# Sparse attention in a two-block transformer on one core: the selection added on VectorE instead of by an identity matmul, and two PSUM banks exchanged

## The reference, cut to what matters

```python
def dsa_attention(q, k, v, iq, ik, iw, rel_bias, topk):      # per block of 128 queries
    score = jnp.einsum('bqhs,bqh->bqs', jax.nn.relu(s_idx), iwb)
    score = jnp.where(keys <= pos_q, score, -jnp.inf)
    _, idx = lax.top_k(score, topk)                           # topk = 128
    ...
    logits = jnp.einsum('bqhd,bqkd->bhqk', qb, kg) * scale
    logits = logits + bias(pos_q - idx)
    p = jax.nn.softmax(jnp.where(valid, logits, -jnp.inf))
    return jnp.einsum('bhqk,bqkd->bqhd', p, vg)
```

## Time and profile before

| | us |
|---|---|
| median of 3 runs (3006.83 to 3009.97) | 3009.62 |
| profiled execution, whole | 3007.83 |
| its span, first to last instruction | 3006.0 |
| TensorE busy (94% of the span) | 2836.8 |
| VectorE busy (36%) | 1091.3 |
| GpSimd busy (37%) | 1103.3 |
| ScalarE busy (31%) | 927.0 |
| mean granted TensorE clock | 0.969 |

### The profile page before, as it was taken

How to read it: one execution, slowest core, us unless ns; L and a number is a source line. 1 busy time by engine, 2 the same in 40 slices (tenths; PEclk the granted TensorE clock), 3 DMA queues, 4 the chain that set the end, 5 groups by cost and what they waited for, 6 DMA issues and landing times.

```text
span 3006.0 us, 34273 instructions
## 1 busy us (share of the span) xinstructions
PE 2836.8 (94%) x13922; PEld 2176.9 (72%) x13922; DVE 1091.3 (36%) x1796; ACT 927.0 (31%) x1425; POOL 1103.3 (37%) x536
## 2 busy tenths in 40 slices
PE   3679999999998997699999999999999999999999
PEld 1167688878877785357887677766788877777787
DVE  2262133113224402322221447854322465666411
ACT  2031241224124211042222322255422222666411
POOL 3043302341341330024554333444455443445443
PEclk8589999999999998799999999999999999999999
DMA  8914722231238320032434233322344333332442
GB/s 293 351 56 145 228 62 61 68 94 41 71 88 130 84 71 28 14 127 74 123 112 99 70 98 85 91 78 85 123 123 119 84 99 91 85 83 76 137 122 81
DMA packets 459337, 311.94 MB, mean 104 GB/s; under 512 B 32016, under 2 KB 412816, under 8 KB 458416
## 3 DMA queue, kind: packets, MB, share of 16 engines
q1 hardware_dynamic: 425264, 265.41, 30.8%
q10 hardware_dynamic: 33920, 44.37, 5.7%
HBM read 289.71 MB, written 32.10 MB: 107 GB/s over the span
## 4 chain that ended last, share of the span: by engine, by line
PE 89%; DMA 4%; DVE 3%; POOL 2%; ACT 1%; issue 1%; SPq 0%; ACTq 0%; DVEq 0%; POOLq 0%
PE acc L1654 75%; PE aux L1654 7%; PE ssq L1657 3%; PE ssq L1654 3%; DMA ada_ring<-in_w_ada 2%; DMA raw<-in_w_in 1%; POOL normed L1042 1%; DVE x_t L1191 1%; DVE rstd L1222 1%; PE aux L1657 1%; POOL w_lo L1053 1%; DMA masks_sb<-in_masks 1%; ACT staged L727 0%; ACT w_hi L748 0%; DVE p L1283 0%
## 5 line engine op out<-in xcount | busy, mean ns | idle before, releaser
L1053 POOL TENSOR_TENSOR w_lo<-raw,w_hi 128x1024 fp32r<-128x1024 f32 x362 | 869.7, 2403 | 1699.7 <-ACT w_hi L748 1699.7
L1654 PE MATMUL acc<-h_hi,w_hi 128*128 128x512 f32 (+1 forms) x3232 | 1211.0, 392 | 23.4 <-DVE x_t L1191 8.0
L1654 PE MATMUL acc<-h_hi,w_lo 128*128 128x512 f32 (+1 forms) x3232 | 1173.2, 380 | 0.0
L1654 PE MATMUL acc<-h_lo,w_hi 128*128 128x512 f32 (+1 forms) x2464 | 873.0, 376 | 0.8 <-issue 0.8
L748 ACT ACTIVATE w_hi<-raw 128x1024 fp32r<-128x1024 f32 x362 | 383.0, 1059 | 1166.2 <-PE acc L1654 1086.2
L1654 PEld LDWEIGHTS acc<-h_hi,w_hi 128*128 128x128 f32 x3232 | 585.7, 188 | 176.4 <-issue 52.3
L1654 PEld LDWEIGHTS acc<-h_hi,w_lo 128*128 128x128 f32 x3232 | 584.2, 188 | 118.1
L1654 PEld LDWEIGHTS acc<-h_lo,w_hi 128*128 128x128 f32 x2464 | 441.1, 189 | 94.7 <-issue 13.0
L1654 PE MATMUL acc<-out_t_lo,w_hi 128*128 128x512 f32 x768 | 298.9, 389 | 0.0
L1222 DVE RECIPROCAL rstd<-rstd 128x512 f32<-128x512 f32 (+1 forms) x29 | 118.0, 4070 | 407.0 <-ACT rstd L788 407.0
L1654 PEld LDWEIGHTS acc<-out_t_lo,w_hi 128*128 128x128 f32 x768 | 144.3, 188 | 29.1
(11 more groups left out here) (217 smaller groups left out, 2341.1 us busy)
## 6 DMA issues: line engine op xcount, KB each, us to landing
raw<-in_w_in SPq DMA_DIRECT2D x52, 1024.0 KB, 5.8
raw<-in_even_w_in SPq DMA_DIRECT2D x41, 1024.0 KB, 5.5
raw<-in_odd_w_in SPq DMA_DIRECT2D x36, 1024.0 KB, 5.6
ada_ring<-in_w_ada SPq DMA_DIRECT2D x32, 1024.0 KB, 8.7
gate_ring<-in_w_ada SPq DMA_DIRECT2D x16, 1024.0 KB, 7.1
raw<-in_w_out SPq DMA_DIRECT2D x16, 1024.0 KB, 5.9
raw<-in_even_w_out SPq DMA_DIRECT2D x16, 1024.0 KB, 5.8
raw<-in_odd_w_out SPq DMA_DIRECT2D x16, 1024.0 KB, 6.6
```

Source lines behind the costliest of these rows:

```text
L1053: G_.tensor_tensor(WL[half][:], RAW[G.rs][:, half * HALF * P:(half + 1) * HALF * P], WH[half][:].bitcast(F32), ALU.subtract).then_inc(S["l ...
L1654: return M.matmul(out_, lhsT, rhs, start=start, stop=stop, skip_group_check=True)
```

## The change

The selection is no longer added on TensorE. The two matmuls with the fp32r identity, the identity's tile `IDR` and its cast go, and `SEL` becomes plain fp32. For qt > 0 VectorE adds the mask to the scores of both heads in one operation, from PSUM and SBUF into `P2`, with a semaphore `d_picked` for which it then waits itself; the two operations of bias and maximum then read `P2` in place of PSUM. For qt = 0 they read PSUM as before. The scores now go to the two banks of `AUX`, and the values product to the upper halves of `ACC`.

```diff
-    V2, IDR = at("v2_nat", QT * 64, 172 * K1), at("ident_r", P, 173 * K1, F32R)
+    V2 = at("v2_nat", QT * 64, 172 * K1)
-    SEL = at("select_mask", 3 * SEQ, 178 * K1, F32R)
+    SEL = at("select_mask", 3 * SEQ, 178 * K1)
...
                     dve.wait_ge(S["d_out"], u + 1)
-                    Vv.tensor_tensor(o, AUX[:, (u % 2) * 512:(u % 2) * 512 + P], o, ALU.mult).then_inc(S["d_fin"], 1)
+                    Vv.tensor_tensor(o, ACC[:, u % 2, 512:512 + P], o, ALU.mult).then_inc(S["d_fin"], 1)
                 if s < 32:
                     j, qt = DSA_UNITS[s]
                     nk = P * (qt + 1)
                     need(dve, "d_turned", 2 * (s - 4) + 2)
+                    if qt:
+                        p = P2[qt][:].rearrange("p (h n) -> p h n", n=nk)
+                        sel = SEL[:, (qt - 1) * SEQ:(qt - 1) * SEQ + nk].unsqueeze(1).to_broadcast([P, 2, nk])
+                        dve.wait_ge(S["d_scored"], 2 * s + 2)
+                        Vv.tensor_tensor(p, AUX[:].rearrange("p (h n) -> p h n", n=512)[:, :, 0:nk], sel, ALU.add).then_inc(S["d_picked"], 1)
+                        dve.wait_ge(S["d_picked"], 3 * j + qt)
                     for half in range(2):
...
-                        Vv.tensor_tensor_reduce(out=P2[qt][:, half * nk:half * nk + nk], in0=ACC[:, half, 512:512 + nk],
+                        p = P2[qt][:, half * nk:half * nk + nk]
+                        Vv.tensor_tensor_reduce(out=p, in0=p if qt else AUX[:, half * 512:half * 512 + nk],
                                                 in1=TR[slot][:, SEQ - nk:SEQ], scale=-1.0, scalar=-NEG, op0=ALU.add,
                                                 op1=ALU.min, accum_out=LNG[:, c:c + 1]).then_inc(S["d_max"], 1)
...
                     elif k == "ikw":
                         dve.wait_ge(S["y_turned"], 1)
-                        L.done(Vv.tensor_copy(IDR[:], IDENT[:]))
...
-                            e = mm(AUX[64 * half:64 * half + 64, (u % 2) * 512:(u % 2) * 512 + P], V2[:, b * 64:b * 64 + 64],
+                            e = mm(ACC[64 * half:64 * half + 64, u % 2, 512:512 + P], V2[:, b * 64:b * 64 + 64],
...
-                    if qt:
-                        pe.wait_ge(S["sel_done"], 1)
-                        for half in range(2):
-                            mm(ACC[:, half, 512:512 + nk], IDR[:], SEL[:, (qt - 1) * SEQ:(qt - 1) * SEQ + nk], True, False)
                     for half in range(2):
                         rows = slice(64 * half, 64 * half + 64)
-                        mm(ACC[:, half, 512:512 + nk], Q2[rows, j * SEQ + qt * P:j * SEQ + (qt + 1) * P], K2[rows, 0:nk],
-                           qt == 0, True).then_inc(S["d_scored"], 1)
+                        mm(AUX[:, half * 512:half * 512 + nk], Q2[rows, j * SEQ + qt * P:j * SEQ + (qt + 1) * P], K2[rows, 0:nk],
+                           True, True).then_inc(S["d_scored"], 1)
```

More of the change, by code:

```diff
@@ L492, in build @@
             "i_scored", "i_relu", "i_acc",
-            "d_scored", "d_max", "d_exp", "d_inv", "d_norm", "d_turned", "d_pt0", "d_pt1", "d_out", "d_fin",
+            "d_scored", "d_picked", "d_max", "d_exp", "d_inv", "d_norm", "d_turned", "d_pt0", "d_pt1", "d_out", "d_fin",
             "w_scored", "w_max", "w_exp", "w_inv", "w_norm", "w_turned", "w_pt0", "w_pt1", "w_out", "w_fin")}
```

## The result

The changed kernel takes 3016.07 us (median of 7 runs, 3012.96 to 3020.16) against 3009.56 us (7 runs). The ratio is 1.0024, 95% interval 1.0013 to 1.0036: about 0.24% slower. A second measurement on another occasion gave 1.0025 (1.0016 to 1.0034).

What follows compares the result with a forecast made beforehand. TensorE bounds the kernel (89% of the chain), with VectorE already last to arrive once per gate group. 5.8 - 4.2 + 8.9 - 0.5 + 1.7 = +11.7 us on the profiled 3007.83 gives 3019.5; stated 3020.5 us, range 3004 to 3033.

Steps and rivals of the forecast that it cites:

- the likeliest case: The forecast itself: VectorE comes late at hooks 12 and 4, 3020.5 us, own range 3016 to 3025, chance 0.47.
- Removal, 1.64 us a group: TensorE's selection matmuls in the eight gate groups go: 13.1 us in all if nothing else were late.
- Hook 8 to hook 12, +0.73: Between a gate group's k-tiles 8 and 12: VectorE's addition and self-wait delay the values product (PV), +5.8 us in all.
- Hook 12 to 16, -0.54: Between a gate group's k-tiles 12 and 16: VectorE has slack, so the removed matmuls count, -4.2 us in all.
- Hook 16 to hook 4, +0.87: From k-tile 16 to the next group's 4: maxima with two SBUF inputs wait for GpSimd; all groups +8.9 us.
- First group, +2.11: Hook 16 to hook 4 in the first gate group, where GpSimd's `w_lo` begins 1.24 us later: +2.11 us.
- a fall of the clock, +1.7: One more fall of the granted clock, behind the first group's new wait of 2.65 us: +1.7 us.
- The cast, -0.5: VectorE's cast of the identity goes, for which TensorE's first index unit was waiting: -0.5 us.
- Banks, 0: PV's results to the upper half of the accumulator banks, scores to `aux`: same waits, 0.
- Rival 1: Hook 16: both maxima run without waiting for GpSimd, -3.5 us in all, 3006 us; chance 0.31.
- Rival 2: Clock also falls at seven of fifteen waits of 1.5 to 1.7 us, 12 us more, 3032 us; chance 0.17.
- Rival 3: The 0.46 us wait at hook 12 is TensorE's own; it gains the whole 13.1 us, 2996 us; chance 0.05.

Runs made afterwards that it cites:

- the version with both edits: Changed kernel with masked scores written back to PSUM and `out_t_lo` moved from ahead of hook 8 to behind hook 12; 2989.07 us, ratio 0.9939 to the kernel before.
- the doubling: Changed kernel with the mask added twice for the qt=1 units (hook 8), the second addition with its own wait; 3028.1 us.
- the second profile: Profile of the changed kernel run once more, nothing altered; 3015.13 us against 3006.91, ratio 1.0025.
- the run of the exchange alone: Kernel before with scores and selection in `aux` and the values product in the upper halves of `acc`, selection still on TensorE; ratio 1.0001.
- the first experiment: Changed kernel with VectorE writing the masked scores back to PSUM instead of SBUF; 3003.66 us against 3007.58, ratio 0.9985.

## Why the prediction was right

The forecast was 3020.5 us and the sum +11.7 (which, added to the median, would have been 3021.3); the kernels differ by 6.5 us in the medians (8.2 in the second measurement), so the sum is 1.4 to 1.8 times what was measured. Of the two medians 3016.07 us lies at the lower end of the likeliest case's own range, 3016 to 3025, and 3015.13 us just below it. The direction, both places and both mechanisms were as forecast. The period grew from 21.75 to 22.48 us, for about 22.8. Step by step:

- *Removal, 1.64 us a group.* Right: with nothing else late the three intervals fall by 1.68 together, from the kernel before with `out_t_lo` moved to the version with both edits.
- *Hook 8 to hook 12, +0.73.* Exact: 5.76 to 6.49 in seven groups, +0.63 in the first (0.65 expected). The price of the addition with its self-wait (0.61 + 0.12) was confirmed twice, by the start of the first maximum 0.71 behind the addition's and by the doubling (+0.73, there with both inputs in SBUF). No run shows its two parts apart.
- *Hook 12 to 16, -0.54.* Measured -0.55, and the slack of 0.9 us was 0.83.
- *Hook 16 to hook 4, +0.87.* The mechanism was right and the size was off: +0.54 in six groups. The forecast let the first maximum wait until `w_lo` ended, +3.65 behind PV; it started at +3.55, before `w_lo`'s recorded end at +3.68, and ran its plain 0.69. GpSimd's product then ended at +5.57 for +5.76, and the copy behind the second maximum started 0.48 behind it, not 0.61. Six times 0.33 is 2.0 us of the 2.7 by which the sum for the stage (12.2) was above the profile (9.5). For the last group 1.23 was measured for 1.56.
- *First group, +2.11 and a fall of the clock, +1.7.* Measured +1.76 (the same term of the sum) and +1.58. Here `w_lo` runs on 1.25 us after the first maximum starts, and both maxima wait, as the forecast had it for every group:

```profile
1981.03 2.41 POOL L1053 TENSOR_TENSOR w_lo<-raw,w_hi 128x1024 fp32r<-128x1024 f32 x1 [3.18 <-ACT w_hi L748]
1982.19 1.80 DVE L1445 CUSTOM_DVE_ANT_0 p<-p,dist_bias 128x512 f32<-128x512 f32 x1
1983.39 1.92 POOL L1103 TENSOR_TENSOR p<-p,u_inv 128x768 f32<-128x768 f32 x1
1983.92 1.94 DVE L1445 CUSTOM_DVE_ANT_0 p<-p,dist_bias 128x512 f32<-128x512 f32 x1
```

- *The term for hook 16 as a whole.* With the first group's 0.35, the last group's 0.33 and the six times 0.33 the whole 2.7 us lie in the term for hook 16. This is the term that was mis-sized. That the fall of the clock came to +1.58 is luck: the same wait had none in the second profile, and the sum had counted as fixed what comes and goes. The fall behind the earlier 2 us wait, in the earlier trace rows, is missing in several runs too, the version with both edits among them.
- *The cast, -0.5.* Measured -0.50.
- *Banks, 0.* Shown by the run of the exchange alone.
- Without the 2.7 us of the mis-sized term and the 1.7 us of the fall the sum is +7.3, between the two differences of the medians (+6.5 and +8.2). How often the clock falls in the executions that were not profiled is not known, and either kernel's times spread by 3 to 7 us, so I can't divide it further.

Rival 1 (no contention for the maxima) fell by the row of 1.95 us and by the first experiment. Rival 2 (more falls of the clock) did not come at waits of up to 1.8 us, 14 of them in each of the two profiles. In the run with the addition doubled at hook 8 it came behind waits of 2.38 us, four times in seven, and behind one of 1.81 us, a length that the changed kernel has too: the case stood nearer to it than the forecast said. Rival 3 fell with the kernel before whose `out_t_lo` was moved.

The rule cited in the prediction, of the Trainium skill, SBUF — State Buffer, section "Who interferes with whom", is borne out for this instruction too: 0.69 us with one input in PSUM, 1.95 us with two in SBUF beside a GpSimd product. What it says on who blocks whom, that the order of issue decides, fits with one addition from the rows: GpSimd's product, waiting behind the first maximum, goes ahead of the second (1.93 and 1.95 us in the fourth group, 1.92 and 1.94 in the first).

## What to carry to other kernels

Before work is moved from the busiest engine to an idle one, look for the places where the busiest engine already waits, even for half a microsecond: there the receiving engine has no slack whatever its busy share says, the removed work isn't earned and the added work is paid in full. The same addition cost 0.73 us at one hook and nothing at the next. And where a result is written decides what its reader contends with: writing it back to PSUM, or preparing it a step earlier, made of a 0.24% loss a gain of 0.6%, together with moving one operation by four k-tiles. When two edits are joined like this, measure each against its own start: the move alone, without the change, was worth 0.16%.

## What the runs showed of the hardware that I had not expected

- A VectorE instruction with two SBUF inputs that started 0.13 us before the recorded end of a GpSimd instruction was not delayed at all (0.69 us); one that started 1.25 us before it took 1.80. The recorded end of GpSimd's work seems to lie behind its last read; that is inferred from this one place, which repeats in the middle groups, and no run tests it.
- Writing a 1024-wide fp32 addition back to the PSUM banks that it reads took 1.23 us, against 1.22 into SBUF.
- The granted clock answers to a wait of 1.8 to 2.4 us sometimes and sometimes not, with the same instructions around it: 0.77 and 1.00 behind two waits of 2.38 us in one execution, and 1.00 behind the one of 3.20 us there. A fall cost 1.4 to 1.6 us where TensorE set the pace, and nothing where it waited for VectorE anyway.
